# Output projection's first panel amid the last pair of heads, its last panel tile by tile, and attention's norms split up, in a two-block transformer kernel on one core

## The chip, the core and the metric

The kernel runs on one core of a Trainium2 chip. The metric is the device time of one execution in microseconds (us). The kernel before takes 2343.22 us (median of three runs, 2342.91 to 2344.21). A core has a matrix engine (TensorE), a vector engine (VectorE), an activation engine (ScalarE), a general engine (GpSimd) and a queue engine for transfers (SyncE). Each works through its own list in order, and they meet only at semaphores. In the profile they are PE, DVE, ACT, POOL and SP.

## The reference, cut to what is computed

Two blocks run one after the other. The first has three kinds of attention heads and a gated feed-forward part. The second, `second_block`, has two layers on 256 latent tokens and 256 context tokens of width 2048: a pooling layer, and a latent-attention (MLA) layer with 16 heads. The change touches the second layer and its norm:

```python
h_lat = rms_norm(x, pre_norm[i]) * (1 + scale[:, None]) + shift[:, None]   # scale, shift, gate: silu(c) @ ada_w + ada_b
...
def mla_project(h, w_in, q_norm, kv_norm, w_uq, w_ukv, rope):
    c_q, c_kv, k_r, gate = jnp.split(h @ w_in, [...], axis=-1)             # 512, 512, 64, 2048
    q = (rms_norm(c_q, q_norm) @ w_uq)                                     # 16 heads of 128 + 64
    kv = (rms_norm(c_kv, kv_norm) @ w_ukv)                                 # 16 heads of 128 + 128
...
s = (q_nope k_nope + q_rope k_rope) * MLA_SCALE                            # keys: context and latent tokens
o_lat = softmax(s) @ v
y_lat = (o_lat * jax.nn.silu(g_l)) @ w_out                                 # 2048 x 2048
x = x + gate[:, None] * rms_norm(y_lat, post_norm[i])
```

## The kernel before

Everything is float32. A product of two float32 tensors is made of three fast matmuls: each operand is split into `hi` (rounded) and `lo` (the rest), and hi x hi, hi x lo and lo x hi are added up in PSUM.

**Weights as one stream.** All weights pass through a ring of four slots (`RING`) in chunks of 256 rows x 512 columns (448 for the MLA input). For each chunk SyncE loads `raw`, ScalarE writes `hi` (`his`, `split_hi`, L552), VectorE writes `lo` (`los`, `split_lo`, L556), and TensorE multiplies with `by_tokens` (L616). `hi` of chunk c waits until chunk c - 4 has been used, and `raw` of chunk c until chunk c - 4 has been split. A panel is 8 chunks (`CH`), 512 output columns. Chunks of the adaLN weights stand between them in the stream; they aren't used by TensorE, but VectorE adds them up itself (`ada_chunk`, L585, four operations each). In the MLA input there are 16 of them, one for every 1.75 weight chunks, from panel 2 to panel 5.

**Norms.** A `Norm` is carried out in steps that stand in the engines' lists: squares with a running sum (`norm_squares`, ScalarE, L703), mean (`norm_mean`, VectorE, L779), power of -0.5 (`norm_root`, GpSimd, L784), product with the root (`norm_apply`, VectorE, L789), transposes (`norm_turn`, TensorE, L805), then scale and shift (ScalarE, L873) and the split into hi and lo (`norm_shift_split`, VectorE, L898 and L905). `parts` divides the token tiles of a norm, of 128 tokens each, into groups that get a mean and a root of their own. `n_mla` is the latents' norm ahead of the MLA input; `n_cq` and `n_ckv` are the norms of the latent queries and keys. Their squares and products stand in the lists of panel 4: in ScalarE's after four chunks, in VectorE's after `mla_los(4, 0, RING)`.

**Heads in pairs.** Eight pairs; the loop interleaves the scores, softmax and values of pair i with the projections of pair i + 1. The last pair has nothing to be interleaved with: transposes of the probabilities (`pair_probs`, L2575), values (`pair_rows`, L2583), product with the gate (`pair_gate`, L2067), transposes (`pair_columns`, L2591), and `om_hi` and `om_lo` (L1558, L2074).

**Output projection.** It is four panels of 8 chunks, whose chunk j takes heads 2j and 2j + 1. TensorE starts it thus:

```python
            pair_columns(PAIRS - 1)
            pe.wait_ge(om_lo_done, FREE + PAIRS)
            for n in range(D // W):
                pe.wait_ge(yout_taken[1], n + 1)
                panel_by_tokens(pe, C_MLA_OUT + n * CH, 0, PLAIN_ORDER, 0, om_hi, om_lo, pair(n % 2), W)
```

Behind each panel ScalarE squares both token tiles out of PSUM (`yout_squares`, L1473) and VectorE multiplies them with the gates (`yout_gated`, L1834), which a transfer has spread over the partitions (L1464). Behind the last panel come the sum and the mean for both tiles (`yout_mean_square`, L1842 and L1844), the root (`yout_roots`, L1175), `x + root * y` for each tile (`yout_join`, L1850) and one store for each tile (L1109).

## Time and profile before

| | us |
|---|---|
| median of the runs | 2343.22 (2342.91 to 2344.21) |
| profiled execution | 2340.59 |
| its span, first to last instruction | 2338.8 |
| TensorE busy in the span | 2282.1 (98%) |
| VectorE busy | 1677.7 (72%) |
| ScalarE busy | 1029.0 (44%) |
| GpSimd busy | 75.9 (3%) |
| mean granted clock of TensorE | 0.995 |

The profile is of one execution. A row of its timeline gives the start and the length of an instruction, or of several alike in sequence (x16), in us from the start of the span, and in brackets how long the engine was idle before it and whom it waited for. Matmuls overlap: the length in a row is longer than the step from one to the next. The granted clock is a share of 2.4 GHz: 1.00 is that level, 0.50 is 1.2 GHz. The TensorE clock was at 1.00 in nearly the whole span; the stretches where it wasn't are short.

### The profile page before, as it was taken

Reading aid. Unit: us, or ns where it says so; the run is one execution under the profiler, and the core shown is the slowest. Engines: PE = TensorE matmul, PEld = TensorE weight load, DVE = VectorE, ACT = ScalarE, POOL = GpSimd, SP = SyncE. Lnnn points to the kernel's source line nnn. Section 1 sums busy time; section 2 is a strip of 40 time slices with the busy share of each in tenths; the row PEclk is TensorE's granted clock in tenths of the full one; section 3 lists DMA queues with packets and bytes.
Section 4 is the critical chain, followed back from the end, with each engine's and each line's share of the span. In section 5 each row is a group of like instructions: output and inputs, shape, how many; then the busy total and the mean of one; then the engine's idle time right before and its main releaser. Section 6 shows DMA issues by size and latency. Waiting matters only on the chain.

```text
span 2338.8 us, 30869 instructions
## 1 busy us (share of the span) xinstructions
PE 2282.1 (98%) x11041; PEld 1888.1 (81%) x11041; DVE 1677.7 (72%) x2394; ACT 1029.0 (44%) x1474; POOL 75.9 (3%) x113
## 2 busy tenths in 40 slices
PE   8999999999999999999999999999999899999997
PEld 6878788877878878777778888888888798999876
DVE  5479876688788877686878675857865878666644
ACT  5565655555556555344352222213322634544432
POOL 1022200000000000000000000000000000000000
PEclk9999999999999999999999999999999999999999
DMA  7966645667677766787756464646654467422243
GB/s 240 217 179 201 186 146 170 187 220 226 214 224 222 225 216 212 232 261 235 253 184 187 146 193 143 195 144 197 225 181 149 121 185 218 129 76 63 73 154 133
DMA packets 225945, 430.33 MB, mean 184 GB/s; under 512 B 13847, under 2 KB 38671, under 8 KB 224688
## 3 DMA queue, kind: packets, MB, share of 16 engines
q1 hardware_dynamic: 222112, 418.96, 58.3%
q10 hardware_dynamic: 3152, 9.83, 1.3%
q8 instruction: 66, 1.08, 0.2%
q14 instruction: 39, 0.32, 0.0%
q0 software_dynamic: 576, 0.14, 0.0%
HBM read 426.16 MB, written 2.72 MB: 183 GB/s over the span
## 4 chain that ended last, share of the span: by engine, by line
PE 68%; issue 18%; DVE 6%; DMA 5%; ACT 3%; DVEq 0%; ACTq 0%; POOL 0%; SPq 0%; POOLq 0%
PE ps L616 40%; PE ps L651 13%; PE ps L628 9%; DMA raw<-in_w_down 3%; DVE ada_acc L585 2%; DVE lo L556 2%; ACT hi L552 1%; DMA raw<-in_w_up 1%; PE ps L2412 1%; PE ps L665 1%; PE ps L2308 1%; DVE ustage L1769 1%; ACT ustage L1342 0%; PE ps L2172 0%; PE ps L805 0%
## 5 line engine op out<-in xcount | busy, mean ns | idle before, releaser
L552 ACT ACTIVATE hi<-raw 128x1024 fp32r<-128x1024 f32 x604 | 634.4, 1060 | 1074.2 <-PE ps L616 536.7
L556 DVE TENSOR_TENSOR lo<-raw,hi 128x1024 fp32r<-128x1024 f32 x604 | 732.0, 1223 | 457.3 <-ACT hi L552 455.1
L585 DVE SCALAR_TENSOR_TENSOR ada_acc<-raw,csil,ada_acc 128x512 f32<-128x512 f32 x720 | 492.4, 748 | 3.5 <-DMA raw<-in_ada_w 3.5
L616 PE MATMUL ps<-hi,h_hi 128*128 128x512 f32 x960 | 382.1, 398 | 2.6 <-DVE lo L556 2.6
L616 PE MATMUL ps<-hi,h_lo 128*128 128x512 f32 x960 | 378.9, 395 | 0.0
L616 PE MATMUL ps<-lo,h_hi 128*128 128x512 f32 x960 | 378.8, 395 | 0.0
L616 PE MATMUL ps<-hi,g 128*128 128x512 f32 x704 | 227.9, 398 | 11.3 <-DVE lo L556 11.2
L616 PEld LDWEIGHTS ps<-hi,h_hi 128*128 128x128 f32 x960 | 180.8, 188 | 46.8 <-DVE lo L556 6.0
L616 PEld LDWEIGHTS ps<-hi,h_lo 128*128 128x128 f32 x960 | 180.8, 188 | 42.3
L616 PEld LDWEIGHTS ps<-lo,h_hi 128*128 128x128 f32 x960 | 180.8, 188 | 40.6
L616 PEld LDWEIGHTS ps<-hi,g 128*128 128x128 f32 x704 | 132.4, 188 | 48.0 <-DVE lo L556 17.6
L651 PE MATMUL ps<-hi,h_hi 128*128 128x512 f32 (+1 forms) x352 | 141.1, 401 | 3.1 <-DVE h_lo L766 3.1
L616 PE MATMUL ps<-lo,g 128*128 128x512 f32 x352 | 138.8, 394 | 0.0
L651 PE MATMUL ps<-hi,h_lo 128*128 128x512 f32 (+1 forms) x352 | 136.3, 387 | 0.0
L651 PE MATMUL ps<-lo,h_hi 128*128 128x512 f32 (+1 forms) x352 | 136.0, 387 | 0.0
L616 PE MATMUL ps<-hi,y_rest 128*128 128x512 f32 x384 | 121.8, 395 | 0.0
L616 PE MATMUL ps<-hi,k_hi 128*128 128x448 f32 (+2 forms) x288 | 103.9, 361 | 5.9 <-DVE lo L556 4.1
L616 PE MATMUL ps<-lo,k_hi 128*128 128x448 f32 (+2 forms) x288 | 102.5, 356 | 0.0
L616 PE MATMUL ps<-hi,k_lo 128*128 128x448 f32 (+2 forms) x288 | 102.3, 355 | 0.0
L628 PE MATMUL ps<-h_hi,hi 128*128 128x512 f32 x256 | 102.0, 398 | 0.0
L628 PE MATMUL ps<-h_lo,hi 128*128 128x512 f32 x256 | 101.0, 395 | 0.0
L628 PE MATMUL ps<-h_hi,lo 128*128 128x512 f32 x256 | 101.0, 395 | 0.0
(328 smaller groups left out, 3430.2 us busy)
## 6 DMA issues: line engine op xcount, KB each, us to landing
raw<-in_ada_w SPq DMA_DIRECT2D x192, 512.0 KB, 4.2
raw<-in_w_up SPq DMA_DIRECT2D x176, 512.0 KB, 4.5
raw<-in_w_down SPq DMA_DIRECT2D x88, 512.0 KB, 5.1
raw<-in_w_in SPq DMA_DIRECT2D x84, 512.0 KB, 4.6
raw<-in_pool_w_in SPq DMA_DIRECT2D x64, 512.0 KB, 4.2
raw<-in_mla_w_in SPq DMA_DIRECT2D x56, 448.0 KB, 3.9
raw<-in_w_out SPq DMA_DIRECT2D x32, 512.0 KB, 3.8
raw<-in_pool_w_out SPq DMA_DIRECT2D x32, 512.0 KB, 4.5
```

What stands on the lines that cost most here:

```text
L552: act.activation(hi[:, slot, :, :], raw[:, slot, :, :], ACT.Copy).then_inc(hi_split, 1 + ada)
L556: dve.tensor_tensor(lo[:, slot, :, :], raw[:, slot, :, :], hi[:, slot, :, :].bitcast(F32), ALU.subtract).then_inc(lo_split, 1)
L585: ins = dve.scalar_tensor_tensor(acc, raw[:, slot, k, :], csil[:, v, kt:kt + 1], acc, ALU.mult, ALU.add)
L616: mm = pe.matmul(ps[:, bank, 0:n], tokens(a, kt0 + k, tok), w[:, slot, k, col0:col0 + n], start=first and k == 0 and s == 0, stop=last and ...
L628: mm = pe.matmul(ps[:, bank0 + n, :], w[:, slot, k, n * P:(n + 1) * P], a[:, kt0 + k, :], start=first and k == 0 and s == 0, stop=last and ...
L651: mm = pe.matmul(ps[:, PAIR * half + tok, 0:width], x, w[:, k, :], start=first and k == 0 and s == 0, stop=last and k == nk - 1 and s == 2)
L665: mm = pe.transpose(ps[:, bank + at * P // W, at * P % W:at * P % W + P], ada_acc[:, a, v, q * P:(q + 1) * P], ident)
L1769: ins = dve.scalar_tensor_tensor(conv[which][:, m, back:SEQ], turned_u(m)[:, 0:SEQ - back], cols[:, bass.ds(ch + vec[0] * P + vec[1], 1)], ...
L2308: mm = pe.transpose(turned_u(m)[:, tok * P:(tok + 1) * P], ustage[:, which, tok, m * P:(m + 1) * P], ident)
L2412: mm = pe.matmul(ps[:, m, s * SEQ + c0:(s + 1) * SEQ], u[:, TT * (1 - s) + k, m * P:(m + 1) * P], poolm[:, bass.ds(n, 1), k, c0:].rearrang ...
```

## The change

It moves work and adds no arithmetic; the product of the weights stays the same.

- TensorE: chunks 0 and 1 of output panel 0 go ahead of the last pair's transposes, chunks 2 and 3 between each two heads' transposes and their values, chunk 4 ahead of the last transposes, chunks 5 to 7 behind them, the wait for `om_lo` only ahead of chunk 7. ScalarE and VectorE split chunks 4 to 7 amid the pair's softmax work.
- The last panel: chunks 0 to 3 for both token tiles, then chunks 4 to 7 for tile 0, then for tile 1. Squares, gate product, sum, root, join and store are done by tile, the join in two halves with a store of 512 KB each.
- `n_mla` gets a mean, a root and a product for each tile.
- `norm_shift_split` makes the first `lo` before the second `hi`.
- The squares, mean and product of `n_cq` move to panel 3; the squares of `n_ckv` are spread between the chunks of panel 4, its mean comes two chunks later, its products are divided in two.

```diff
@@ -899,10 +899,12 @@
             for g in range(n.groups):
-                if g + 1 < n.groups:
+                if 0 < g < n.groups - 1:
                     high(g + 1)
                 dve.wait_ge(n.hi_done, n.groups0 + g + 1)
                 dve.tensor_tensor(part(n.lo, g), copy(g), part(n.hi, g).bitcast(F32), ALU.subtract).then_inc(n.lo_done, 1)
+                if g == 0:
+                    high(1)
@@ -991,9 +993,9 @@
                  k4_lo[s][:, :, :], KT, lambda k, _, s=s: hscale[:, s, k:k + 1],
-                 lambda k, _, s=s: adat[:, 1, k, s:s + 1], shift_tmpb, banks=banks)
-            for s, src, banks in ((LAT, [xres[:, i, :] for i in range(TT)], (4, 5, 0, 1)),
-                                  (CTX, [yout[i][:, :] for i in range(TT, NT)], (4, 5, 6, 7))))
+                 lambda k, _, s=s: adat[:, 1, k, s:s + 1], shift_tmpb, banks=banks, parts=parts)
+            for s, src, banks, parts in ((LAT, [xres[:, i, :] for i in range(TT)], (4, 5, 0, 1), [(i, i + 1) for i in range(TT)]),
+                                         (CTX, [yout[i][:, :] for i in range(TT, NT)], (4, 5, 6, 7), None)))
@@ -1105,9 +1107,11 @@
             for i in range(TT):
-                sp.wait_ge(yout_added[1], i + 1)
-                sp.dma_start(out[0, i * P:(i + 1) * P, :], xres[:, i, :]).then_inc(out_stored, 16)
-            sp.wait_ge(out_stored, 16 * TT)
+                for half in range(2):
+                    sl = slice(half * D // 2, (half + 1) * D // 2)
+                    sp.wait_ge(yout_added[1], 2 * i + half + 1)
+                    sp.dma_start(out[0, i * P:(i + 1) * P, sl], xres[:, i, sl]).then_inc(out_stored, 16)
+            sp.wait_ge(out_stored, 16 * TT * 2)
@@ -1175,12 +1179,16 @@
             yout_roots(0, LAT)
-            norm_root(pool, n_mla)
+            for i in range(TT):
+                norm_root(pool, n_mla, i)
             yout_roots(0, CTX)
             norm_root(pool, n_mla_ctx)
             norm_root(pool, n_cq)
             norm_root(pool, n_ckv)
-            yout_roots(1, LAT)
+            for i in range(TT):
+                pool.wait_ge(yout_mean[1], i + 1)
+                _, mean, root = (v[:, i:i + 1] for v in y_stats[1])
+                pool.tensor_tensor(root, mean, halves[:, 0:1], ALU.pow).then_inc(yout_root[1], 1)
@@ -1490,7 +1498,8 @@
             his(act, C_MLA, 0, 0, 0, 1)
-            norm_squares(act, n_mla, lambda e, i: e.wait_ge(yout_added[0], i + 1), 0, lat_junk[:, :])
+            for i in range(TT):
+                norm_squares(act, n_mla, lambda e, i: e.wait_ge(yout_added[0], i + 1), i, lat_junk[:, :])
@@ -1511,16 +1520,21 @@
                     mla_his(p, 5, CH)
+                elif p == 4:
+                    act.wait_ge(n_cq.squared, n_cq.rows0 + TT)
+                    for m in range(NT):
+                        mla_his(p, m, m + 1)
+                        norm_squares(act, n_ckv, lambda e, i: e.wait_ge(mla_taken, PAIR + 4) if i < TT else e.wait_ge(mla_ctx_taken, 2),
+                                     0, lat_junk[:, 0:W], [m])
+                    mla_his(p, NT, CH)
                 else:
                     mla_his(p, 5 if p == 1 else 0, RING + int(p == 1))
                     if p == 0:
                         mla_his(0, RING, CH)
                         act.wait_ge(n_mla.lo_done, n_mla.all_groups)
                         norm_squares(act, n_mla_ctx, lambda e, i: e.wait_ge(yout_added[0], i + 1 + TT), 0, ctx_junk[:, :])
-                    if p == 4:
-                        norm_squares(act, n_cq, lambda e, i: e.wait_ge(mla_ctx_taken, 2))
-                        act.wait_ge(n_cq.squared, n_cq.rows0 + TT)
-                        norm_squares(act, n_ckv, lambda e, i: None)
+                    if p == 3:
+                        norm_squares(act, n_cq, lambda e, i: e.wait_ge(mla_taken, PAIR + 3), 0, lat_junk[:, 0:W])
@@ -1567,12 +1581,16 @@
             pair_exps(PAIRS - 1)
+            his(act, C_MLA_OUT, 0, 0, RING, 2 * RING)
             pair_out(PAIRS - 1)
             gates_from_dram(1)
             for n in range(D // W):
-                his(act, C_MLA_OUT + n * CH, 0, 0, RING, RING + CH)
+                his(act, C_MLA_OUT + n * CH, 0, 0, RING if n else 2 * RING, RING + CH)
+                if n == D // W - 1:
+                    act.wait_ge(lat_summed, 2)
+                    yout_squares(1, n, 2 * (n % 2), slice(0, 1))
                 act.wait_ge(chunks_used, used(C_MLA_OUT + (n + 1) * CH))
-                yout_squares(1, n, 2 * (n % 2))
+                yout_squares(1, n, 2 * (n % 2), slice(int(n == D // W - 1), TT))
@@ -1948,9 +1966,11 @@
                 yout_join(0, tok, xres[:, tok, :], xres[:, tok, :])
+            norm_mean(dve, n_mla, 0)
             los(dve, C_MLA, 0, 0, 0, 1)
-            norm_mean(dve, n_mla)
-            norm_apply(dve, n_mla)
+            norm_mean(dve, n_mla, 1)
+            for i in range(TT):
+                norm_apply(dve, n_mla, i)
@@ -1971,21 +1991,26 @@
             for p in (2, 3):
-                mla_los(p, 0, CH)
+                mla_los(p, 0, RING + 2)
+                if p == 3:
+                    norm_mean(dve, n_cq)
+                mla_los(p, RING + 2, CH)
+                if p == 3:
+                    norm_apply(dve, n_cq)
                 n = MLA_ORDER[p]
                 dve.wait_ge(chunks_used, used(C_MLA + mla_at(p + 1, 0)))
                 col0, w = CTX_COLS[n]
                 to = n * W_IN + col0 - Q_RANK
                 dve.tensor_copy(proj_c[:, :, to:to + w], ps[:, 2 + 2 * n:4 + 2 * n, 0:w])\
                    .then_inc(mla_ctx_taken, 1)
-            mla_los(4, 0, RING)
-            norm_mean(dve, n_cq)
+            mla_los(4, 0, RING + 1)
             norm_mean(dve, n_ckv)
-            norm_apply(dve, n_cq)
-            norm_apply(dve, n_ckv)
-            mla_los(4, RING, RING + 2)
+            mla_los(4, RING + 1, RING + 2)
+            norm_apply(dve, n_ckv, 0, range(TT))
             take_ada(dve, ADA_MLA, 6)
-            mla_los(4, RING + 2, CH)
+            mla_los(4, RING + 2, RING + 3)
+            norm_apply(dve, n_ckv, 0, range(TT, NT))
+            mla_los(4, RING + 3, CH)
@@ -2096,17 +2121,34 @@
             pair_max(PAIRS - 1)
-            for ms in ((0, 1), (2, 3)):
+            for half, ms in enumerate(((0, 1), (2, 3))):
                 pair_turned(PAIRS - 1, ms)
+                los(dve, C_MLA_OUT, 0, 0, RING + half, RING + half + 1)
                 pair_gate(PAIRS - 1, ms)
+            los(dve, C_MLA_OUT, 0, 0, RING + 2, 2 * RING)
             pair_out_lo(PAIRS - 1)
             dve.wait_ge(gates_loaded, 16 * 3)
             for n in range(D // W):
-                los(dve, C_MLA_OUT + n * CH, 0, 0, RING, RING + CH)
-                yout_gated(1, n, 2 * (n % 2))
-            yout_mean_square(1, LAT)
+                los(dve, C_MLA_OUT + n * CH, 0, 0, RING if n else 2 * RING, RING + CH)
+                if n < D // W - 1:
+                    yout_gated(1, n, 2 * (n % 2))
+
+            def out_row(i):
+
+                total, mean, root = (v[:, i:i + 1] for v in y_stats[1])
+                yout_gated(1, D // W - 1, 2, slice(i, i + 1))
+                dve.reduce_sum(total, panel_sums[:, i:i + 1, :], AX_X).then_inc(yout_summed[1], 1)
+                dve.wait_ge(yout_summed[1], i + 1)
+                dve.tensor_scalar(mean, total, 1.0 / D, EPS, ALU.mult, ALU.add).then_inc(yout_mean[1], 1)
+                dve.wait_ge(yout_taken[1], PAIR + D // W + i)
+                dve.wait_ge(yout_root[1], i + 1)
+                for half in range(2):
+                    sl = slice(half * D // 2, (half + 1) * D // 2)
+                    dve.scalar_tensor_tensor(xres[:, i, sl], YOUT[1][i][:, sl], root, xres[:, i, sl], ALU.mult, ALU.add)\
+                       .then_inc(yout_added[1], 1)
+
             for i in range(TT):
-                yout_join(1, i, xres[:, i, :], xres[:, i, :])
+                out_row(i)
@@ -2615,14 +2657,36 @@
                 pair_scores(i + 1)
-            for ms in ((0, 1), (2, 3)):
+
+            def out_part(n, j, outs, frees=True):
+                at = C_MLA_OUT + n * CH + j
+                return by_tokens(pe, at, at % RING, om_hi, om_lo, CK_T * j, outs, W, j == 0, j == CH - 1, 0, frees)
+
+            pe.wait_ge(yout_taken[1], 1)
+            for j in range(2):
+                out_part(0, j, pair(0))
+            for half, ms in enumerate(((0, 1), (2, 3))):
                 pair_probs(PAIRS - 1, ms)
+                out_part(0, 2 + half, pair(0))
                 pair_rows(PAIRS - 1, ms)
+            out_part(0, 4, pair(0))
             pair_columns(PAIRS - 1)
-            pe.wait_ge(om_lo_done, FREE + PAIRS)
-            for n in range(D // W):
+            for j in range(5, CH):
+                if j == CH - 1:
+                    pe.wait_ge(om_lo_done, FREE + PAIRS)
+                out_part(0, j, pair(0))
+            for n in range(1, D // W - 1):
                 pe.wait_ge(yout_taken[1], n + 1)
                 panel_by_tokens(pe, C_MLA_OUT + n * CH, 0, PLAIN_ORDER, 0, om_hi, om_lo, pair(n % 2), W)
+            n = D // W - 1
+            pe.wait_ge(yout_taken[1], n + 1)
+            for j in range(RING):
+                out_part(n, j, pair(1))
+            for j in range(RING, CH):
+                mm = out_part(n, j, pair(1)[0:1], False)
+            mm.then_inc(lat_summed, 1)
+            for j in range(RING, CH):
+                out_part(n, j, pair(1)[1:TT])
```

Beside this, `norm_squares` and `norm_apply` take a list of tiles, `rows`, that replaces the part's own tiles.

## Rows read from the trace of the kernel before

**Rows 1.** Windows: stretch, length, busy of five engines, clock, DMA share, GB/s.

```profile
1824.00:1842.00 18.00, 13.72 (x79) 12.03 (x79) 14.33 (x22) 12.99 (x25) 0.00 (x0) 1.00 0.28 80
...
1872.00:1940.00 68.00, 68.00 (x384) 64.71 (x384) 47.75 (x63) 19.82 (x21) 0.00 (x0) 1.00 0.62 187
...
2226.00:2228.00 2.00, 2.00 (x11) 2.00 (x10) 0.39 (x2) 0.00 (x0) 0.00 (x0) 0.50 0.03 8
```

**Rows 2.** Timeline, TensorE, last pair: start, length, instruction, idle before.

```profile
2221.75 0.40 PE L2567 MATMUL ps<-kr_hi,qr_lo 64*128 64x512 f32 x2
...
2225.53 3.64 PE L2583 MATMUL ps<-v_sb,mprobs_t 128*128 128x128 f32 x16 [0.85 <-DVE mprobs_t L2059]
...
2235.01 0.50 PE L616 MATMUL ps<-hi,om_hi 128*128 128x512 f32 x1 [1.41 <-DVE om_lo L2074]
```

**Rows 3.** Timeline, TensorE, the same steps in the loop, a pair earlier.

```profile
2203.42 1.95 PE L2583 MATMUL ps<-v_sb,mprobs_t 128*128 128x128 f32 x16
2205.20 1.04 PE L2575 MATMUL ps<-ident,mprobs 128*128 128x128 f32 x8
2205.99 0.48 PE L2522 MATMUL ps<-ckv_hi,hi 128*128 128x512 f32 x1
```

**Rows 4.** Timeline, ScalarE and VectorE, splits of output chunks 4, 5 and 11.

```profile
2239.72 1.06 ACT L552 ACTIVATE hi<-raw 128x1024 fp32r<-128x1024 f32 x1 [5.49 <-PE ps L616]
...
2240.89 1.23 DVE L556 TENSOR_TENSOR lo<-raw,hi 128x1024 fp32r<-128x1024 f32 x1 [5.93 <-ACT hi L552]
...
2242.52 1.06 ACT L552 ACTIVATE hi<-raw 128x1024 fp32r<-128x1024 f32 x1 [1.74 <-PE ps L616]
...
2259.32 1.06 ACT L552 ACTIVATE hi<-raw 128x1024 fp32r<-128x1024 f32 x1 [1.74 <-PE ps L616]
```

**Rows 5.** DMA issues, 2220 to 2339: count, KB each, median us to landing.

```profile
raw<-in_mla_w_out SPq DMA_DIRECT2D x26, 512.0 KB, 3.6
out<-xres SPq DMA_DIRECT2D x2, 1024.0 KB, 4.0
gate_rows<-gates ACTq DMA_DIRECT2D x1, 1024.0 KB, 4.6
```

**Rows 6.** Timeline, all engines, behind the last matmul.

```profile
2326.47 0.60 ACT L1473 ACTIVATE yout<-ps 128x512 f32<-128x512 f32 x1 [10.08 <-PE ps L616]
...
2327.19 1.29 DVE L1834 TENSOR_TENSOR yout<-ps,gate_rows 128x512 f32<-128x512 f32 x2 [9.54 <-ACT yout L1473]
...
2328.83 0.70 POOL L1175 TENSOR_TENSOR rstd<-ms,halves 128x2 f32<-128x2 f32 x1 [367.63 <-DVE ms L1844]
...
2329.63 4.62 DVE L1850 SCALAR_TENSOR_TENSOR xres<-yout,rstd,xres 128x2048 f32<-128x2048 f32 x2 [0.88 <-POOL rstd L1175]
```

**Rows 7.** Timeline, start of the MLA input; one later root.

```profile
1823.85 2.48 DVE L789 TENSOR_SCALAR yout<-xres,rstd 128x2048 f32<-128x2048 f32 x2 [0.81 <-POOL rstd L784]
...
1829.00 0.43 DVE L898 CAST k_hi<-shift_tmpb 128x512 fp32r<-128x512 f32 x1 [0.48 <-ACT shift_tmpb L873]
1829.34 0.68 DVE L905 TENSOR_TENSOR k_lo<-shift_tmpb,k_hi 128x512 fp32r<-128x512 f32 x1
...
1830.08 0.48 PE L616 MATMUL ps<-hi,k_hi 128*128 128x448 f32 x1 [1.84 <-DVE k_lo L905]
...
1847.45 1.61 POOL L1175 TENSOR_TENSOR rstd<-ms,halves 128x2 f32<-128x2 f32 x1 [23.64 <-DVE ms L1844]
```

**Rows 8.** Timeline, VectorE and TensorE, MLA input, panel 4.

```profile
1956.63 2.74 DVE L585 SCALAR_TENSOR_TENSOR ada_acc<-raw,csil,ada_acc 128x512 f32<-128x512 f32 x4
...
1960.26 1.86 DVE L789 TENSOR_SCALAR proj_l<-proj_l,rstd 128x512 f32<-128x512 f32 x4 [0.40 <-POOL rstd L784]
...
1964.09 0.74 PE L616 MATMUL ps<-hi,k_hi 128*128 128x448 f32 x1 [3.53 <-DVE lo L556]
...
1969.49 0.38 PE L616 MATMUL ps<-hi,k_lo 128*128 128x448 f32 x1
1969.70 0.36 PE L616 MATMUL ps<-hi,k_hi 128*128 128x448 f32 x1
```

8 lines of the change are left out of this document (4 added, 4 removed).

## The prediction, made before the change was built

> **What bounds the kernel now.** I read the page's busy shares first (TensorE busy 98% of the span, VectorE 72%), then the stages: where TensorE is busy throughout, as in 1872 to 1940, only fewer matmuls help [rows 1], so an edit is worth just the idle and slow-clock time of TensorE in its own stage. The timeline of TensorE shows such time in four places that this change touches: around the last pair of heads, after the last matmul, at the start of the attention's input projection (panel 0), and in that projection's panel 4. Everything between them is dense, so what is won in one place is kept to the end.
>
> Last pair. Its last score matmul starts at 2221.75 and frees TensorE at 2222.0; panel 0 of the output projection starts at 2235.01 [rows 2]. In between come 16 transposes and 32 value matmuls, each group waiting for a softmax step of ScalarE or VectorE. The first 16 value matmuls take 3.64 us [rows 2]; in the loop, where other matmuls fill the gaps, 16 take 1.78 (2203.42 to 2205.20) and 8 transposes 0.79 (2205.20 to 2205.99) [rows 3]. The rest of the excess is clock: the grant is 0.50 at 2226 to 2228 [rows 1], the 1.2 GHz level. ScalarE's hi copies, each released by a used chunk, tell the pace of panel 0: chunk 0 is used at 2239.7, and from there one chunk takes 2.80 us [rows 4]; chunk 0 itself took 4.65.
>
> **The change part by part.**
>
> **A, output panel 0 amid the last pair.** The same instructions in another order: chunks 0 and 1, transposes, chunk 2, values, transposes, chunk 3, values, chunk 4, four transposes, chunks 5 to 7. Chunk j reads heads 2j and 2j+1, so only chunk 7 needs the last pair. Weight chunks 0 to 3 are split by then (the loop's last turn does it). Before: 2222.0 to 2259.25 (chunk 7 used, the last row of [rows 4]), 37.25 us. After, if nothing waits: 8 x 2.80 + 2 x 0.79 + 2 x 1.78 + 0.4 for four transposes = 27.95. Does anything wait? From TensorE at 2222.0: chunk 1 ends at 2227.6, transposes 2228.4, chunk 2 2231.2, values 2233.0, transposes 2233.8, chunk 3 2236.6, values 2238.4, chunk 4 2241.2, transposes 2241.6, chunk 5 2244.4, chunk 6 2247.2, chunk 7 2250.0. The splits of chunks 4 to 7 stand in ScalarE's queue (1.06 each, then om_hi) and VectorE's (1.23 each [rows 4]). hi(4) waits for chunk 0 and is done by 2226.6; lo(4) comes behind two copies on VectorE, done by 2231, needed at 2238.4. hi(7) waits for chunk 3 (2236.6), done 2237.8, and om_hi is queued behind it, but its transposes end only at 2241.6. lo(7) ends at 2241.1, om_lo at 2243.2, needed at 2247.2. The gates' load is issued behind om_hi at 2242.5, lands 4.6 later [rows 5], and VectorE waits for it ahead of lo(8): 2248.3, needed at 2250.0. That 1.7 us is the thinnest cover; its loss costs what exceeds it. The largest of the kernel's three such loads would land 0.4 too late by my count. So **9.3 us**, bounds 8.5 and 9.4.
>
> **B, last panel token by token.** The matmul count stays. Token tile 0 is complete 4 x 1.40 = 5.6 us before the end, and its square, gate product, sums, root and join (0.8 + 0.6 + 0.3 + 1.0 + 2.3 = 5.0 by [rows 6]) hide under tile 1's matmuls; if they did not, tile 1's join would be late by the excess. For tile 1, from the last matmul at T = 2326.43: before, the gate products start at T+0.76, the joins at T+3.20, and they end at T+7.85 [rows 6]. After: one product less (0.6) and one join less (2.3): T+4.95. The last store is 512 instead of 1024 KB; stores of 1024 took 4.0 us [rows 5]. For the half size I take 3.6, what the loads of 512 KB take [rows 5]; the bounds are no gain (4.0) and half (2.0). **3.3 us**, bounds 2.9 and 4.9. The Trainium skill (DMA: Bandwidth & Descriptors, Anatomy of one DMA) gives a fixed part of some 2.0 us for each DMA; by it the store would land in an estimated 3.0 and B would be 3.9. No row here separates the two.
>
> **C, the norm of the input split by tile.** Mean, root and product are now made for each token tile. Before, both products (1.2 each, 2.48 together [rows 7]) start at 1823.85 behind one root; now product 0 can start at 1823.0, right after mean 1, since root 0 was made during the join's end and a split. Product 1 needs root 1, which GpSimd starts at 1823.15, while product 0 runs. Such a root takes 0.70 on a quiet VectorE [rows 6], but 1.61 where it met a running VectorE split at 1847.45 [rows 7]. With 0.70, product 1 starts at 1824.2 and the transposes 0.85 earlier, less 0.1 for the one transpose that no longer runs ahead: 0.75 gain. Held back, root 1 ends at 1824.9 and product 1 starts at 1824.95 against 1825.05: nothing after that 0.1. I take 0, since the only row with both engines running says so; bounds 0 and 0.75. The Trainium skill (GPSIMD Engine Reference, Key points) speaks against this edit in the same way: GpSimd shares its SBUF interfaces with VectorE and contends with two-port modes and two-input instructions. The row of 1.61 agrees.
>
> **D, first lo ahead of the second high.** VectorE made high(0), waited 0.48 for ScalarE, made high(1), and only then lo(0) at 1829.34, for which TensorE started at 1830.08 after 1.84 idle [rows 7]. Now lo(0) starts 0.34 after high(0), 1828.43: **0.9 us**. Later groups follow TensorE's own transposes behind chunk 0, so they shift with it. In the other two uses of the helper TensorE showed no wait for the first lo that a later wait would not take back: 0.
>
> **E, norms of the latent queries and keys spread.** Before, VectorE did both norms in one lump in panel 4 (products 1.86 + 0.88, 0.40 waiting for the root), and TensorE stood still 3.53 us until 1964.09; after that it ran 14 matmuls in 5.40 us, to 1969.49, at a step of some 0.38 against the 0.21 that follows [rows 8]. 448 columns in 0.37 is the 1.2 GHz level. At the other step, 0.205, they would take 2.9: 2.5 more. At most 6.0 to win. But the work isn't gone. VectorE does an adaLN chunk (four operations, 2.74 as listed, 2.65 from start to start) for every 1.75 weight chunks (1.14 from start to start), 4.65 us, while TensorE needs 1.75 x 12 x 0.205 = 4.3 [rows 8]: VectorE is the bound from the end of panel 3 to the last adaLN chunk, with or without the lump. The query product (0.93) now stands behind panel 3's last split, still in that stretch; only the waits for squares and root go. Following the queues with these durations: chunk 6 of panel 4 is ready at 1961.3, wanted at 1960.5 (0.8 idle); panel 5's chunk 1 waits about 0.7 and its chunk 2 until 1974.2, where it started at 1977.3. So three stalls of 0.6 to 1.4 us stand in for one of 3.5 and its slow clock: **3.0 us**, bounds 0.5 (the clock falls anyway) and 6.0.
>
> Other edits cost nothing: squares written to SBUF instead of PSUM, 0.8 each, lie in ScalarE's idle time; the number of roots on GpSimd grows by a few of 0.7, beside work, save root 1 of C.
>
> **Sum:** 9.3 + 3.3 + 0 + 0.9 + 3.0 = 16.5 us. The profiled execution took 2340.59 (span 2338.8, 1.8 around it) and would take 2324.1. The runs' median, 2343.22, lies 2.6 above it; I carry that over: 2343.2 - 16.5 = **2326.7**.
>
> **Rivals.**
> 1. *VectorE stays the bound in panel 4 and the clock still falls* (E is worth 0.5). For it: the three small stalls come within 15 us. Against it: from 1824 to 1842 TensorE was idle for 4.3 us in three or more pieces, the longest 1.84, at a grant of 1.00 [rows 1, 7]. 2329.2.
> 2. *The gates or a ring slot come late in A*: panel 1 then starts on a wait that replaces the removed one, or chunks 4 to 7 on a late split. With 3 us lost: 2329.7. Against it: 1.7 us is the thinnest cover.
> 3. *All upper bounds* (roots not held back, no stall in panel 4, short last store): 0.75 + 3.0 + 1.6 more, 2321.4.
> 4. *Slower than before*: the low clock takes hold in the interleaved stage. The one mechanism of this size: short value matmuls and transposes between the chunks keep the grant at 0.50, as for 2226 to 2228. 512 columns at 1.2 GHz take 0.43 instead of 0.23 (2.80 for 12), 0.19 more. From 16.5 / 0.19 = 87 matmuls on, the change loses; all 96 of panel 0 and the slower short ones (5.5 more) would give 2343.2 - 16.5 + 18.6 + 5.5 = 2350.8. Against it: the loop mixes the same kinds densely, at full step [rows 3].
> 5. *The change doesn't do what it says*: TensorE waits in order, so if its first wait (a free bank pair) or the weights are late, the panel moves nowhere: A is 0, 2336.0. The weights were split before the last scores, so I give it little.
>
> **How the numbers follow.** Forecast 0.66; rival 1 0.13, rival 2 0.08, rival 3 0.09, rival 4 0.02, rival 5 0.02. The range reaches over rivals 1 and 2 and part of the way to 3: 2322.5 to 2331.0. A measurement of this kernel can tell about 0.2%, 4.7 us. Only rival 4 is on the slower side, none stands within 4.7 us: faster 0.96, same 0.02, slower 0.02.
>
> **What would show each step.** A: output panel 0's first matmul at about 2222 less what came before, no idle of TensorE above 0.3 us until panel 1, granted clock 1.00 in the stage, ScalarE's hi(8) at 20.8 us behind the last score. B: last join 5.0 us behind the last matmul, the end another 3.6 to 4.5 behind it. C and D: first matmul of panel 0 at 1829.2; at 1828.4 if the root isn't held back. E: no idle above 2 us and no clock below 1.00 between panel 3 and 5. The prediction is wrong if the clock falls in E or in A, or if a wait above 2 us shows at panel 1.

## The result and the profile after

| | before, us | after, us |
|---|---|---|
| median of the runs side by side | 2343.06 (2341.62 to 2344.21, 4 runs) | 2326.22 (2324.15 to 2329.5, 4 runs) |
| profiled execution | 2340.59 | 2328.25 |
| its span | 2338.8 | 2326.3 |
| last score of the heads to last matmul (A) | 104.28 | 96.11 |
| last matmul to end of the span (B) | 12.77 | 8.41 |
| last matmul of the first layer's output to first MLA matmul (C, D) | 6.30 | 5.36 |
| first transpose of the context's norm to the first matmul behind the latent queries' transposes (E) | 117.05 | 114.60 |

The ratio after to before is 0.9933, with a 95% interval of 0.992 to 0.9945. That is 15.7 us less, between 12.9 and 18.7. The forecast was 2326.7 us, 16.5 less. The lower rows of the table are from start of instruction to start of instruction on TensorE; the same four stretches are measured in every run below. The span is read to 0.1 us, so the row (B), and the column "end" below, are good to 0.05 us.

The page of the kernel after, first lines: the span, then busy time, share of the span and count for each engine.

```profile
span 2326.3 us, 30882 instructions
...
PE 2280.8 (98%) x11041; PEld 1887.8 (81%) x11041; DVE 1677.0 (72%) x2399; ACT 1028.3 (44%) x1474; POOL 79.6 (3%) x115
```

Busy time is that of before within 1.3 us for TensorE and 0.7 for VectorE. No work was saved. What the change took away is idle time and low clock of TensorE.

**The last pair, TensorE of the kernel after** (start, length, instruction, idle before). It answers to [rows 2].

```profile
2221.78 0.39 PE L2609 MATMUL ps<-kr_hi,qr_lo 64*128 64x512 f32 x2
2222.11 0.50 PE L616 MATMUL ps<-hi,om_hi 128*128 128x512 f32 x1
...
2227.78 1.04 PE L2617 MATMUL ps<-ident,mprobs 128*128 128x128 f32 x8
...
2231.44 1.95 PE L2625 MATMUL ps<-v_sb,mprobs_t 128*128 128x128 f32 x16
...
2241.45 0.60 PE L2633 MATMUL ps<-ident,om 128*128 128x128 f32 x4
...
2251.11 0.47 PE L616 MATMUL ps<-hi,om_hi 128*128 128x512 f32 x1 [0.66 <-DVE lo L556]
```

The output projection now starts 0.33 behind the last score; before, it started 13.26 behind. No row between has an idle note. The 16 values are one group of 1.95 us, as in the loop [rows 3], and not 3.64 as in [rows 2]. Their windows (stretch, length, busy of five engines, granted clock, DMA share, GB/s) show the clock, which was 0.50 at 2226 to 2228 before [rows 1]:

```profile
2222.00:2251.00 29.00, 28.45 (x150) 23.66 (x148) 13.35 (x27) 11.47 (x17) 0.00 (x0) 1.00 0.41 143
```

The last row of the timeline above has what is left: 0.66 us idle at panel 1.

**The end, all engines of the kernel after.** It answers to [rows 6].

```profile
2315.12 2.48 DVE L2147 SCALAR_TENSOR_TENSOR xres<-yout,rstd,xres 128x1024 f32<-128x1024 f32 x2 [0.73 <-POOL rstd L1191]
...
2318.31 0.60 ACT L1481 ACTIVATE yout<-ps 128x512 f32<-128x512 f32 x1 [4.89 <-PE ps L616]
2319.03 0.69 DVE L1852 TENSOR_TENSOR yout<-ps,gate_rows 128x512 f32<-128x512 f32 x1 [1.43 <-ACT yout L1481]
2320.05 0.55 POOL L1191 TENSOR_TENSOR rstd<-ms,halves 128x1 f32<-128x1 f32 x1 [5.04 <-DVE ms L2142]
2320.71 2.48 DVE L2147 SCALAR_TENSOR_TENSOR xres<-yout,rstd,xres 128x1024 f32<-128x1024 f32 x2 [0.73 <-POOL rstd L1191]
```

The last matmul starts at 2317.89. Tile 0's joins are the first row and had ended by 2317.6, so only tile 1's two halves (2.48 together) stand behind the last matmul; before, two whole tiles stood there (4.62).

**Start of the MLA input, all engines of the kernel after.** It answers to [rows 7].

```profile
1823.93 1.46 POOL L784 TENSOR_TENSOR rstd<-ms,halves 128x1 f32<-128x1 f32 x1 [4.87 <-DVE ms L779]
1825.93 1.28 DVE L789 TENSOR_SCALAR yout<-xres,rstd 128x2048 f32<-128x2048 f32 x1
1826.09 1.53 POOL L784 TENSOR_TENSOR rstd<-ms,halves 128x1 f32<-128x1 f32 x1 [0.70 <-DVE ms L779]
1826.72 0.39 PE L616 MATMUL ps<-hi,y_rest 128*128 128x512 f32 x1
1827.65 1.29 DVE L789 TENSOR_SCALAR yout<-xres,rstd 128x2048 f32<-128x2048 f32 x1 [0.45 <-POOL rstd L784]
1829.09 3.04 PE L805 MATMUL ps<-ident,yout 128*128 128x128 f32 x16 [1.98 <-DVE yout L789]
...
1832.08 0.74 PE L616 MATMUL ps<-hi,k_hi 128*128 128x448 f32 x1
```

Root 1 starts while VectorE makes product 0 and takes 1.53 us, and product 1 waits 0.45 for it. The last matmul of the layer ahead starts at 1826.72; before, at 1823.78. These 2.94 us arise far ahead of the change (below, under the offset).

**Panels 4 and 5, TensorE of the kernel after, every row with idle time.** They answer to [rows 8].

```profile
1955.11 0.47 PE L616 MATMUL ps<-hi,k_hi 128*128 128x448 f32 x1 [0.17 <-DVE lo L556]
1963.81 0.47 PE L616 MATMUL ps<-hi,k_hi 128*128 128x448 f32 x1 [0.23 <-DVE lo L556]
1969.68 0.44 PE L616 MATMUL ps<-hi,k_hi 128*128 128x448 f32 x1 [0.71 <-DVE lo L556]
1972.65 0.47 PE L616 MATMUL ps<-hi,k_hi 128*128 128x448 f32 x1 [0.29 <-DVE lo L556]
1977.22 0.47 PE L616 MATMUL ps<-hi,k_hi 128*128 128x448 f32 x1 [1.00 <-DVE lo L556]
```

Five waits of 2.4 us together, all for VectorE's split, stand where one of 3.53 us stood. The windows of the same kernel have no low clock:

```profile
1945.00:1965.00 20.00, 19.60 (x105) 17.54 (x104) 17.92 (x24) 9.73 (x15) 0.00 (x0) 1.00 0.75 235
1965.00:1980.00 15.00, 13.00 (x66) 11.18 (x65) 14.44 (x20) 6.65 (x7) 1.44 (x1) 1.00 0.74 221
```

VectorE is busy 17.9 of 20 and 14.4 of 15 us in them.

**The account of the two spans.** 8.17 (A) + 4.36 (B) + 0.94 (C and D) + 2.45 (E) = 15.92 gained. Given back: 2.94 ahead of the MLA layer, 0.45 between the first MLA matmul and the context's transposes (30.09 before, 30.54 after), 0.03 in the long stretch of heads. 15.92 - 3.42 = 12.5 = 2338.8 - 2326.3. The medians moved by 16.8. The difference lies in the two executions that the profiler happened to record: that of before was 2.5 below its median, that of after 2.0 above.

### The profile page after: what moved, and what is told of

Read it like the earlier page. It is cut to its first block, busy times and chain, and to the rows that moved or that the text cites. A ratio compares the mean times of both kernels' runs of the same rounds, so it can differ in the third digit from the quotient of the medians.

```text
span 2326.3 us, 30882 instructions
## 1 busy us (share of the span) xinstructions
PE 2280.8 (98%) x11041; PEld 1887.8 (81%) x11041; DVE 1677.0 (72%) x2399; ACT 1028.3 (44%) x1474; POOL 79.6 (3%) x115
## 3 DMA queue, kind: packets, MB, share of 16 engines
q8 instruction: 66, 1.08, 0.2%
## 4 chain that ended last, share of the span: by engine, by line
PE 81%; DVE 7%; DMA 6%; ACT 3%; issue 3%; SPq 0%; POOL 0%; DVEq 0%; ACTq 0%; POOLq 0%
PE ps L616 45%; PE ps L651 13%; PE ps L628 9%; DMA raw<-in_w_down 4%; DVE ada_acc L585 2%; DVE lo L556 2%; PE ps L2589 2%; PE ps L2564 2%; ACT hi L552 1%; PE ps L2625 1%; DMA raw<-in_w_up 1%; PE ps L2603 1%; PE ps L2454 1%; PE ps L665 1%; PE ps L2350 1%
```

## The experiments

The parts bear the letters of the prediction. The first group applies one part alone to the kernel before, the second changes one thing in the kernel after. In the tables, "in" is last matmul of the first layer's output to first MLA matmul, "cq" is first transpose of the context's norm to first matmul behind the latent queries' transposes, "heads" is last score to last matmul, "end" is last matmul to end of the span.

### One part at a time

**A alone.** Only the order of the last pair and output panel 0, with the splits that go with it:

```diff
+            pe.wait_ge(yout_taken[1], 1)
+            for j in range(2):
+                out_part(0, j, pair(0))
...
-            for n in range(D // W):
+            for n in range(1, D // W):
                 pe.wait_ge(yout_taken[1], n + 1)
```

> Only edit A (output panel 0 amid the last pair) on the kernel before. My theory: the stage between the last score matmul and panel 1's first matmul shrinks from 37.3 to 29.1 us as in the changed kernel, with one idle of some 0.7 us in front of panel 1, where VectorE waits for the gates' load; time 8.2 us less than before. Rival, that the stage is worth 9.3 (the gates land in 4.6 when nothing else differs): 28.0 us and no idle at panel 1. Rival, that the other edits carry part of it: under 6 us. Panel 4 of the MLA input is as before here, so TensorE should stand still 3.5 us there and run at the 1.2 GHz level behind it, if that is caused by the idle time and not by chance.

**B alone.** Only the last panel by token tile, with squares, sums, roots, joins and stores by tile:

```diff
+            for j in range(RING):
+                out_part(n, j, pair(1))
+            for j in range(RING, CH):
+                mm = out_part(n, j, pair(1)[0:1], False)
+            mm.then_inc(lat_summed, 1)
+            for j in range(RING, CH):
+                out_part(n, j, pair(1)[1:TT])
```

> Only edit B (last panel's token tiles one behind the other, joins and stores in halves). My theory: from the start of the last matmul to the end of the span 8.4 us instead of 12.8, of which the join's end comes 2.9 earlier and the last store lands 1.4 faster, since it is 512 KB and not 1024; time 4.4 us less than before. Rival: the store's size is worth only 0.4 and the rest of the gain was the run's luck, 3.3 us less. The last pair is as before: 37.3 us from its last score to panel 1.

**E alone.** Only `n_cq` in panel 3 and `n_ckv` spread over panel 4:

```diff
-            mla_los(4, 0, RING)
-            norm_mean(dve, n_cq)
+            mla_los(4, 0, RING + 1)
             norm_mean(dve, n_ckv)
-            norm_apply(dve, n_cq)
-            norm_apply(dve, n_ckv)
-            mla_los(4, RING, RING + 2)
+            mla_los(4, RING + 1, RING + 2)
+            norm_apply(dve, n_ckv, 0, range(TT))
```

> Only edit E (norms of the latent queries and keys spread over panels 3 and 4). My theory, VectorE is the bound there: the idle of 3.5 us and the slow clock go and small idle times of 2.4 us in all take their place, the grant stays 1.00; the way from panel 3's end to panel 5's chunk 2 is 2.5 to 3.0 us shorter; time 2.5 to 3 less. Rival 1, the clock falls all the same: 0.5 less. Rival 2, the lump was the whole cause: no idle left in panels 4 and 5, 6 us less.

**D alone.** Only the first `lo` ahead of the second high:

```diff
-                if g + 1 < n.groups:
+                if 0 < g < n.groups - 1:
                     high(g + 1)
...
+                if g == 0:
+                    high(1)
```

> Only edit D (first lo ahead of the second high). My theory: the first matmul of the MLA input starts 0.9 us earlier against the last matmul of the layer before (5.4 instead of 6.3 us behind it), the idle in front of it 0.9 instead of 1.8, all else as before. Rival, that the second high or ScalarE delays the first lo in the same way: under 0.3 us. The slow clock in that place, seen in the changed kernel, would be chance if it shows here or not without a difference of idle time.

**C alone.** Only the tile-wise norm of the MLA input:

```diff
+            norm_mean(dve, n_mla, 0)
             los(dve, C_MLA, 0, 0, 0, 1)
-            norm_mean(dve, n_mla)
-            norm_apply(dve, n_mla)
+            norm_mean(dve, n_mla, 1)
+            for i in range(TT):
+                norm_apply(dve, n_mla, i)
```

> Only edit C (mean, root and product of the latents' norm for each token tile). My theory: GpSimd's root of tile 1 is held back by VectorE's product 0 and takes 1.5 us (0.7 in the kernel before, where VectorE waits for it), so product 1 starts at most 0.4 us earlier than before and the first matmul of the MLA input 5.9 to 6.3 us behind the last matmul of the layer before (6.3 before). Rival, no contention: root 0.7 or less, first matmul 5.5 us behind it.

Measured:

| kernel | time, us | kernel before beside it | ratio | in | cq | heads | end |
|---|---|---|---|---|---|---|---|
| A alone | 2335.45, 10 runs | 2342.31, 25 runs | 0.9974 (0.9965 to 0.9984) | 6.35 | 116.14 | **96.06** | 12.80 |
| B alone | 2336.91, 10 runs | 2342.31 | 0.9981 (0.9971 to 0.9992) | 6.30 | 116.03 | 102.39 | **8.49** |
| E alone | 2338.38, 10 runs | 2342.31 | 0.9983 (0.997 to 0.9997) | 6.42 | **114.18** | 104.25 | 12.79 |
| D alone | 2346.02, one run | 2342.31 | | **5.50** | 117.37 | 103.95 | 12.74 |
| C alone | 2340.18, one run | 2344.64, one run | | **6.08** | 116.01 | 103.93 | 12.71 |

Each part moves its own stretch. Where its own edit is missing, a stretch still differs by up to 1.9 us ("heads") and 1.4 us ("cq") between traces. The idle times in these traces agree within 0.2 us; most of the difference is how long the clock was low. For "heads", the first 8 us of output panel 0 in the kernel before, at 0.79 with 28 matmuls, and in B alone, at 1.00 with 34:

```profile
2235.00:2243.00 8.00, 7.99 (x28) 6.38 (x29) 1.23 (x1) 1.54 (x2) 0.00 (x0) 0.79 0.28 115
```

```profile
2236.00:2244.00 8.00, 7.99 (x34) 6.51 (x35) 2.18 (x2) 2.12 (x2) 0.00 (x0) 1.00 0.40 153
```

By the ratios, A, B and E alone are worth 6.1 (3.7 to 8.2), 4.5 (1.9 to 6.8) and 4.0 us (0.7 to 7.0), 14.6 together. With the 1.0 of C and D from the "in" column that makes 15.6, against 15.7 measured for all at once: within these intervals, each 4.5 to 6.3 us wide, the parts add up. The times of C and D alone say nothing: D alone took 3.7 us more than the median of before although its own stretch is 0.8 shorter. One run of this kernel can't resolve a microsecond, while the stretch around the edit can.

A alone, the row of DMA issues (count, KB, median us to landing), and the window from 1 to 9 us behind its last score (2226.94). Before, the low clock of [rows 1] stood 4 to 6 us behind the last score:

```profile
gate_rows<-gates ACTq DMA_DIRECT2D x1, 1024.0 KB, 7.6
```

```profile
2228.00:2236.00 8.00, 8.00 (x40) 6.59 (x40) 4.31 (x11) 4.71 (x10) 0.00 (x0) 1.00 0.26 86
```

B alone has the old order in the last pair, and the low clock with it:

```profile
2228.00:2230.00 2.00, 2.00 (x12) 2.00 (x11) 0.36 (x2) 0.00 (x0) 0.00 (x0) 0.50 0.00 0
```

The same difference shows in panel 4 of these kernels. A alone and B alone have the old norms and the stall of 3.5 us, and their clock falls behind it; in E alone both are gone. Windows of A alone, then of E alone:

```profile
1972.00:1976.00 4.00, 4.00 (x15) 3.58 (x13) 4.00 (x6) 1.06 (x1) 0.00 (x0) 0.61 0.78 246
```

```profile
1964.00:1978.00 14.00, 12.37 (x62) 10.57 (x61) 13.48 (x18) 6.40 (x7) 1.24 (x1) 1.00 0.74 230
```

D alone, VectorE and TensorE at the start of the input. The first `lo` follows its `hi` at once, without the copy that stood between them in [rows 7], and TensorE waits 1.05 instead of 1.84:

```profile
1834.35 0.43 DVE L898 CAST k_hi<-shift_tmpb 128x512 fp32r<-128x512 f32 x1 [0.62 <-ACT shift_tmpb L873]
1834.82 0.69 DVE L905 TENSOR_TENSOR k_lo<-shift_tmpb,k_hi 128x512 fp32r<-128x512 f32 x1
1835.56 0.48 PE L616 MATMUL ps<-hi,k_hi 128*128 128x448 f32 x1 [1.05 <-DVE k_lo L905]
```

C alone, GpSimd and VectorE. Root 1 takes 1.53 us beside product 0, and product 1 waits for it:

```profile
1824.07 1.53 POOL L784 TENSOR_TENSOR rstd<-ms,halves 128x1 f32<-128x1 f32 x1 [0.70 <-DVE ms L779]
1825.63 1.29 DVE L789 TENSOR_SCALAR yout<-xres,rstd 128x2048 f32<-128x2048 f32 x1 [0.45 <-POOL rstd L784]
```

### One thing at a time in the kernel after

**The join of a tile as one, with one store.** This asks how B's last 4.4 us divide between joins and store:

```diff
-                for half in range(2):
-                    sl = slice(half * D // 2, (half + 1) * D // 2)
+                for half in range(1):
+                    sl = slice(0, D)
```

> The changed kernel, but with one join and one store of 1024 KB for each token tile instead of halves. My theory: a store's time to landing goes by its size, 4.0 us at 1024 KB against 2.7 at 512 KB, so from the last matmul to the end it is 9.8 us instead of 8.4. Rival, landing does not depend on the size and is short in the changed kernel because tile 0's stores are long done: 8.4 us still, landing 2.7 to 3.0.

**A quarter of VectorE's adaLN work in the MLA input.** This asks whether VectorE is what the stalls in panels 4 and 5 wait for in the end. The kernel leaves out three quarters of the columns of these sums:

```diff
+                    part = slice(0, W // 4 if isinstance(c, int) and C_MLA <= c < C_HEADS else W)
+                    acc = acc[:, part]
...
-                        ins = dve.scalar_tensor_tensor(acc, raw[:, slot, k, :], csil[:, v, kt:kt + 1], acc, ALU.mult, ALU.add)
+                        ins = dve.scalar_tensor_tensor(acc, raw[:, slot, k, part], csil[:, v, kt:kt + 1], acc, ALU.mult, ALU.add)
```

> The changed kernel, but the adaLN operations amid the MLA input's chunks are done on a quarter of their columns (128 of 512), so the sums behind gate and scale are left incomplete; all instructions, waits and loads stay. My theory, VectorE's work bounds panels 3 to 5: an adaLN chunk takes 1.1 us instead of 2.65, and the five small idle times (2.4 us in all) go, at most 0.3 left; from the first transposes of the context norm to the end of the query norm's transposes 112.3 us or less instead of 114.6. Rival, the ring bounds it (a load starts only when the chunk four earlier is split and takes 4 us to land): idle times of 1.5 us or more stay, with ScalarE waiting for loads in front of them.

**The gates loaded before the last pair.** This asks whether the 0.66 us at panel 1 hang on that load:

```diff
+            gates_from_dram(1)
             pair_exps(PAIRS - 1)
             his(act, C_MLA_OUT, 0, 0, RING, 2 * RING)
             pair_out(PAIRS - 1)
-            gates_from_dram(1)
```

> The changed kernel with the load of the gates issued ahead of the last pair's exponentials, 20 us earlier. My theory: the idle of 0.66 us in front of panel 1 was this load's landing (7.6 us among the weights' loads instead of 4.6); it goes, and with it 0.8 us from last score to last matmul (96.1 to 95.3). Rival, a late split of chunk 8 for another reason (its raw or its hi): the idle stays and the waiting row names ScalarE or a weight load.

**Norm products on ScalarE.** Those of `n_cq`, of `n_ckv` and of tile 0 of `n_mla` leave VectorE. This asks both for the stalls in panel 4 and for the root of C, which then meets a quiet VectorE. The product of `n_cq` also moves, from the end of panel 3 into panel 4:

```diff
+            norm_apply_act(act, n_mla, 0, range(1))
...
+                        if m == 1:
+                            norm_apply_act(act, n_cq, 0, range(TT))
...
-            for i in range(TT):
-                norm_apply(dve, n_mla, i)
+            norm_apply(dve, n_mla, 1)
...
-                if p == 3:
-                    norm_apply(dve, n_cq)
```

where `norm_apply_act` is `act.activation(out, src, ACT.Identity, scale=rstd)` for each tile.

> The changed kernel with products moved from VectorE to ScalarE: those of the latent queries' and keys' norms (2.7 us of VectorE's work in panels 3 and 4) and token tile 0's of the latents' norm. My theory: VectorE's work bounds panels 3 to 5 and its product 0 held back GpSimd's root, so the five idle times there fall from 2.4 to under 1 us (from the first transposes of the context norm to the end of the query norm's transposes about 113 instead of 114.6), root 1 takes 0.7 instead of 1.5 and product 1 starts 0.8 us earlier against mean 1, the first matmul of the MLA input about 4.6 us behind the last matmul of the layer before. Rival, the ring's loads bound panels 3 to 5: idle times as before within 0.5 us.

**Both of the last two together, and the kernel after once more beside it.**

> products_scalar and the early load of the gates together. My theory: some 3 us less than the changed kernel (0.8 for the gates, 1.6 in panels 4 and 5, 0.8 at the start of the MLA input), 2323 against 2326. Rival: the slow-clock stretches come and go from run to run by more than that, and the medians lie within 1.5 us of each other.

> The changed kernel again, in the same rounds as the one before. My theory: its time spreads over 2322 to 2332 with where the 1.2 GHz stretches fall; the stages of the change keep their length: 96.1 us from last score to last matmul, 8.4 from there to the end, idle of 2.0 to 2.5 us in panels 4 and 5. Its gain over the kernel before is 15 to 17 us.

Measured:

| kernel | time, us | in | cq | heads | end | idle of TensorE in "cq" | idle at panel 1, landing of the gates |
|---|---|---|---|---|---|---|---|
| after | 2326.22, 4 runs | 5.36 | 114.60 | 96.11 | 8.41 | 2.4 in 5 | 0.66, 7.6 |
| whole join | 2328.66, one run | 5.29 | 114.32 | 96.83 | **9.49** | 2.1 in 5 | 1.39, 8.3 |
| quarter adaLN | 2323.69, one run | 5.36 | **110.93** | 96.91 | 8.47 | **none** | 1.48, 8.4 |
| gates early | 2321.66, one run | 5.30 | 114.12 | **95.18** | 8.42 | 1.9 in 5 | **none, 4.8** |
| products on ScalarE | 2323.21, one run | **4.33** | **112.07** | 96.93 | 8.44 | 0.5 in 1 | 1.50, 8.4 |
| both | 2320.55, 6 runs | 4.39 | 112.64 | 95.47 | 8.43 | 1.1 in 1 | none, 4.9 |
| after, again | 2324.04, 5 runs | 5.35 | 114.22 | 96.22 | 8.44 | 2.0 in 5 | 0.54, 7.5 |

*The store.* DMA issues, first of the kernel with the whole join, then of the kernel after:

```profile
out<-xres SPq DMA_DIRECT2D x2, 1024.0 KB, 3.9
```

```profile
out<-xres SPq DMA_DIRECT2D x4, 512.0 KB, 2.7
```

The half size lands 1.2 us sooner, and the end comes 1.08 later with the whole join (9.49 against 8.41); the whole join itself takes 2.35 us, the two halves 2.48. The expectation had 9.8. So of B's 4.36 us, 2.9 are the earlier end of the last join (5.30 instead of 8.22 us behind the start of the last matmul) and the other 1.4 the store.

*The stalls of panel 4.* With three quarters of the adaLN columns gone, VectorE has time, and TensorE has no idle at all in panels 4 and 5. What is left of waiting lies elsewhere and reaches TensorE no more. The waits of that kernel between 1942 and 1980 (who waited, for whom: us in all, times, longest), all engines:

```profile
ACT hi L552 <- DMA raw<-in_mla_w_in: 11.0, 7, 2.3
DVE lo L556 <- ACT hi L552: 8.7, 8, 2.6
```

So VectorE set the pace there, and not the order of the norm's steps, the roots or the weight loads, which are all still in place. 114.60 - 110.93 = 3.67 us still hang on VectorE in the kernel after, 2.4 of them as TensorE's own idle time. The other 1.3 stand in no idle note. Start by start, the two traces part only at the five matmuls that wait and the one behind each: 0.24 to 0.28 us there beyond each idle note. A note counts from the end of the matmul before, and a matmul is longer (0.4) than the step to the next (0.2). Moving the six products of these norms to ScalarE, which removes no arithmetic, wins most of it (112.07), and one wait is left of five.

*The root.* In the kernel with products on ScalarE, VectorE does nothing while root 1 is made:

```profile
1824.40 0.55 POOL L784 TENSOR_TENSOR rstd<-ms,halves 128x1 f32<-128x1 f32 x1 [0.70 <-DVE ms L779]
1824.98 1.29 DVE L789 TENSOR_SCALAR yout<-xres,rstd 128x2048 f32<-128x2048 f32 x1 [0.67 <-POOL rstd L784]
```

0.55 instead of 1.53 us, and the stretch "in" falls by 1.03 us to 4.33. The root is the same, only its neighbour differs. (The first product runs beside it on another engine now, which may be a part of the gain; the two weren't separated.)

*The gates.* In the kernel after SyncE issues two weight loads just ahead of the gates' load, which is ScalarE's. The queues of SyncE and ScalarE, kernel after:

```profile
2240.51 0.37 SPq L538 DMA_DIRECT2D raw<-in_mla_w_out  x1
2241.65 0.37 SPq L538 DMA_DIRECT2D raw<-in_mla_w_out  x1
```

```profile
2242.10 0.33 ACTq L1472 DMA_DIRECT2D gate_rows<-gates  x1
```

Its DMA engines in three windows behind that are 0.99, 0.79 and 0.96 busy:

```profile
2242.00:2244.00 2.00, 2.00 (x11) 1.59 (x10) 0.69 (x1) 1.66 (x2) 0.00 (x0) 1.00 0.99 303
2244.00:2246.00 2.00, 2.00 (x10) 1.64 (x9) 0.00 (x0) 1.05 (x1) 0.00 (x0) 1.00 0.79 238
2246.00:2248.00 2.00, 2.00 (x11) 1.59 (x10) 0.00 (x0) 0.26 (x2) 0.00 (x0) 1.00 0.96 392
```

VectorE waits for the landing 6.33 us ahead of the split of panel 1's chunk 0:

```profile
2249.74 4.63 DVE L556 TENSOR_TENSOR lo<-raw,hi 128x1024 fp32r<-128x1024 f32 x4 [6.33 <-DMA gate_rows<-gates]
```

Issued before the pair's exponentials, at 2212.42, the load finds its DMA engines empty and lands in 4.8 us. Windows of that kernel, the one ahead of the issue and the one with it:

```profile
2210.00:2212.00 2.00, 2.00 (x19) 2.00 (x19) 0.69 (x1) 0.04 (x1) 0.00 (x0) 1.00 0.00 0
2212.00:2214.00 2.00, 2.00 (x11) 1.65 (x10) 1.82 (x2) 1.82 (x2) 0.00 (x0) 1.00 0.40 66
```

```profile
gate_rows<-gates ACTq DMA_DIRECT2D x1, 1024.0 KB, 4.8
```

The idle at panel 1 is gone, and the stretch "heads" is 0.9 shorter than in the kernel after, 1.7 shorter than in the three kernels where the load took 8.3 or 8.4.

*Both together* took 2320.55 us (2317.55 to 2327.86) where the kernel after took 2324.04 (2321.81 to 2327.17) in the same rounds. Against the kernel before, the ratios are 0.9921 (0.9908 to 0.9934) and 0.9932 (0.9919 to 0.9945). The two intervals overlap, so the runs don't show for certain that it is faster. The stretches say 0.96 + 1.58 + 0.75 = 3.3 us for "in", "cq" and "heads", which is what the medians say too (3.5). The expectation had 3 us between the two kernels, and both 2 to 2.5 us higher than they came out.

## Why the prediction was right

The sum was 16.5 us. Against the two profiled executions each term is in the table of the account; since a stretch differs a little from execution to execution, the means over all traces with and without a part are the better measure:

| part | forecast (bounds) | before and after | means over the traces |
|---|---|---|---|
| A | 9.3 (8.5 to 9.4) | 8.17 | 103.76 (5 without) - 96.51 (6 with, gates late) = 7.25 |
| B | 3.3 (2.9 to 4.9) | 4.36 | 12.76 (5) - 8.44 (7) = 4.32 |
| C and D | 0 + 0.9 | 0.94 | 6.34 (4) - 5.33 (5) = 1.01 |
| E | 3.0 (0.5 to 6.0) | 2.45 | 116.52 (5) - 114.29 (5) = 2.23 |
| sum | 16.5 | 15.9 | 14.8 |

The mechanisms were those of the forecast in all five parts. Three terms were mis-sized, in opposite directions: A and E too large, B too small.

**A: right in its mechanism, too large by 1 to 2 us.** The walk through the queue held within 0.3 us down to the last transposes: first transposes forecast at 2227.6 and seen at 2227.78, second at 2233.0 and 2233.22, last at 2241.2 and 2241.45. The clock stayed at 1.00, so rival 4 fell at once. The step that failed is the cover of the gates' load, "lands 4.6 later". That row of before [rows 5] was of a load that no other transfer met: SyncE issued nothing between 2228 and 2242 there. The change itself filled this silence, since chunks that are split earlier free their slots earlier, and their refills are issued at 2240.51 and 2241.65. The term read 4.6 and measured 7.6 (8.4 in others), the spare 1.7 became a debt of 0.66 (up to 1.50). That is rival 2 at a fifth to a half of its price of 3. The lowest bound, 8.5, was too high for the same reason. It allowed for the largest of the three loads of gates, and that one (6.7 us) had less company: a load of the same size issued 0.36 us ahead of it. In the means the rest of the shortfall comes from the stretch without A, which was 104.28 in the profile that the forecast used and 102.39 in its shortest. Its six waits are the same in both within 0.01 us. The forecast's profile had a second low-clock stretch, at the start of output panel 0, and B alone had not (the two windows above): some 1.4 of the 1.9 us arise there. The 4.65 us of chunk 0, against 2.80 for the others, were mostly this clock, and the forecast counted them as A's gain.

**B: right in the instructions, too small by 1 us in the store.** The last join ends at 2320.71 + 2.48, which is 5.30 behind the start of the last matmul and 4.90 behind its end, the T of the forecast, which had T + 4.95. Before, it was 8.22 by the first measure, so the joins gave 2.9 as forecast. Tile 0's tail was hidden under tile 1's matmuls as worked out. The term that was mis-sized is the landing of the last store: I took 3.6, from loads of the same size; it measured 2.7. A load of 512 KB in this stage has company (3.8 in median after, 26 of them); the last store has only the other half's, issued 1.2 us ahead of it. A store also goes the other way, so the runs don't show that company alone makes the difference. The Trainium skill's estimate of 3.0 (DMA: Bandwidth & Descriptors, Anatomy of one DMA) was nearer, and B would have been 3.9 by it; that section is on transfers that GpSimd issues, and this one is SyncE's. 512 KB more cost 1.2 us (3.9 - 2.7), so by these two points the part that doesn't go by size is an estimated 1.5, where the page has 2.0.

**C and D: right.** Product 0 starts 0.79 ahead of the last matmul of the layer before it, 0.78 by the forecast. Then the root is held back, as the row of 1.61 in [rows 7] said: 1.53 us in C alone and in the kernel after, 0.55 with VectorE quiet. The Trainium skill's rule (GPSIMD Engine Reference, Key points), that GpSimd contends with VectorE for its SBUF interfaces, spoke for the same, and here 1.0 us of root stand behind it. C alone gave 0.2 for the forecast 0, D alone 0.8 for 0.9.

**E: right in its mechanism, 0.6 to 0.8 too large.** VectorE is the bound from the end of panel 3, with or without the lump: the quarter adaLN shows that. The forecast named three stalls of 0.6 to 1.4; there were five, of 0.17, 0.23, 0.71, 0.29 and 1.00, 2.4 in sum. The gain was yet smaller than 3.0, because the forecast read one of the longer stretches: without E it runs from 116.01 to 117.37 in five traces, and it had 117.05. This is the clock again: behind the stall it was low about twice as long in the two longest (before and D alone) as in the other three. The clock stayed at 1.00 in all eight traces with E and fell in all five without, so rival 1 fell.

**The offset.** I added 2.6 us, the distance of the profiled execution of before from its median, as if it belonged to the kernel. It belongs to the execution. In unchanged code far ahead of the change there are stretches at 1.2 GHz that some executions have and others don't. Windows of the kernel after:

```profile
164.00:168.00 4.00, 3.68 (x12) 3.01 (x13) 4.00 (x7) 2.44 (x8) 0.00 (x0) 0.51 0.76 211
...
240.00:248.00 8.00, 8.00 (x47) 6.51 (x46) 5.00 (x9) 2.97 (x8) 0.74 (x2) 0.79 0.60 191
```

The first is in every trace but those of before and C alone. The second is in this trace and in the second recording of the same kernel, and in no other. Matmul by matmul, the kernel after falls 3.1 us behind the trace of before between 164 and 171, and 1.6 us between 242 and 247; all the rest up to the MLA layer takes 1.7 us back. So these two stretches are where the 2.94 us given back above come from, and the lack of the first is a part of why that execution of before lay low. The start of the last matmul ahead of the MLA layer lies between 1822.1 and 1830.1 in the thirteen traces, with the same code up to there, but for D's order in the pooling layer's norm. To subtract from the median was right; to carry the distance from the profile over as a part of the kernel was not. By the means the terms were off by +2.0 (A), -1.0 (B), -0.1 (C and D) and +0.8 (E), 1.7 too much in sum, and the medians of four runs happened to lie 16.8 apart. (In the later rounds they lay 16.4 apart, 2340.40 in 11 runs and 2324.04 in 5, at a ratio of 0.9932.) That the forecast came within 0.5 us is therefore chance in its last 2 us. What the runs support is each term within about 2 us, and a sum of 14.8 to 15.9 for 16.5.

## What to carry to other kernels

Take a transfer's time from a row in which the queues are as full as the change will leave them: an earlier split refills the ring earlier, and a side load that was alone before then shares its way (4.6 became 7.5 to 8.4 us); issue such a load where the DMA share is zero. Where a stall waits for an engine that is nearly full over the whole stage, spreading its work wins the low clock behind the stall and little of the idle time, and only taking work off that engine wins the rest (five waits became one when six products moved to ScalarE). Measure parts worth under 5 us by the stretch between two instructions around them, and over several traces, since one run of 2340 us scatters by more than each of them.
